# Three of four feed-forward blocks by seven half-size products, masks on VectorE, and a 72-row key tile

## The reference

```python
hm = rms_norm(h, g_mlp[l])                                              # first stack
h = h + jnp.square(jax.nn.relu(hm @ w_mlp_in[l])) @ w_mlp_out[l]
...
f = jnp.square(jax.nn.relu(h @ w_ff1[l])) @ w_ff2[l]                    # second stack
x = x + rms_norm_2(f, g_post_ffn[l])
...
mask = qi[:, None] >= k_idx[None, :]                                    # first stack's attention
s = jnp.where(mask, s, -jnp.inf)
...
logits = jnp.einsum('bqhd,bsd->bqhs', iqb, ik32) * (IDX_DIM ** -0.5)    # second stack's index
score = jnp.einsum('bqh,bqhs->bqs', iwb, jax.nn.relu(logits))
```

## Time and profile before

| | us |
|---|---|
| median of 3 runs | 2446.92 (2445.26 to 2449.81) |
| the profiled execution, whole | 2444.17 |
| its span, first to last instruction | 2442.4 |
| PE busy | 2388.9 (98% of the span), 11562 matmuls |
| DVE busy | 1342.5 (55%) |
| ACT busy | 900.2 (37%) |
| POOL busy | 350.1 (14%) |
| granted TensorE clock, mean | 0.996 |

### The profile page before, as it was taken

The page is one execution under the profiler, slowest core; times in us unless marked ns, Lnnn a source line. Parts: engine busy times, 40 slices in busy tenths (PEclk is TensorE's granted clock), DMA queues, the critical chain, the costliest instruction groups (busy, mean ns, idle before and its releaser), DMA issues.

```text
span 2442.4 us, 29077 instructions
## 1 busy us (share of the span) xinstructions
PE 2388.9 (98%) x11562; PEld 1937.8 (79%) x11562; DVE 1342.5 (55%) x1992; ACT 900.2 (37%) x1307; POOL 350.1 (14%) x270
## 2 busy tenths in 40 slices
PE   8998999999999899999999999999999999999997
PEld 6877888888887688888876878888886787888886
DVE  7765433445777643334578866334357975533433
ACT  4555332234455532223433364233233245321331
POOL 2002000002200200000146621000012742000002
PEclk9999999999999999999999999999999999999999
DMA  4211222222322123222222221222231211222221
GB/s 158 104 61 69 90 100 93 97 104 87 102 89 76 68 92 104 86 103 87 104 79 73 79 74 57 100 103 89 100 120 57 70 70 70 84 89 103 89 100 52
DMA packets 33181, 215.58 MB, mean 88 GB/s; under 512 B 4144, under 2 KB 4400, under 8 KB 8112
## 3 DMA queue, kind: packets, MB, share of 16 engines
...
## 4 chain that ended last, share of the span: by engine, by line
PE 89%; DVE 6%; ACT 2%; POOL 1%; issue 1%; DMA 0%; POOLq 0%; SPq 0%; DVEq 0%; ACTq 0%
PE ps L427 81%; DVE wl L367 1%; DVE gl L649 1%; PE ps L2257 1%; PE ps L2212 1%; PE ps L2290 1%; PE ps L2268 1%; PE ps L1390 1%; PE ps L607 1%; PE ps L1414 1%; PE ps L1377 1%; PE ps L310 1%; ACT wh L361 1%; POOL wl L408 0%; DMA wr<-in_weights 0%
## 5 line engine op out<-in xcount | busy, mean ns | idle before, releaser
L427 PE MATMUL ps<-gh,wh 128*128 128x512 f32 x1488 | 590.0, 396 | 14.0 <-DVE gl L649 11.2
L427 PE MATMUL ps<-gl,wh 128*128 128x512 f32 x1488 | 581.4, 391 | 0.0
L427 PE MATMUL ps<-gh,wl 128*128 128x512 f32 x1488 | 581.3, 391 | 0.0
L427 PE MATMUL ps<-hh,wh 128*128 128x512 f32 x1456 | 574.6, 395 | 3.4 <-ACT arena L965 1.1
L361 ACT ACTIVATE wh<-wr 128x2048 fp32r<-128x2048 f32 x184 | 351.0, 1908 | 595.1 <-PE ps L427 594.4
L427 PE MATMUL ps<-hh,wl 128*128 128x512 f32 x1456 | 567.0, 389 | 0.0
L427 PE MATMUL ps<-hl,wh 128*128 128x512 f32 x1456 | 566.8, 389 | 0.0
L367 DVE TENSOR_TENSOR wl<-wr,wh 128x2048 fp32r<-128x2048 f32 x168 | 387.0, 2304 | 278.6 <-ACT wh L361 276.4
L427 PEld LDWEIGHTS ps<-gh,wh 128*128 128x128 f32 x1488 | 279.9, 188 | 82.6 <-DVE gl L649 12.7
L427 PEld LDWEIGHTS ps<-hh,wh 128*128 128x128 f32 x1456 | 272.6, 187 | 69.4 <-issue 8.7
L427 PEld LDWEIGHTS ps<-gh,wl 128*128 128x128 f32 x1488 | 279.8, 188 | 60.0
...
## 6 DMA issues: line engine op xcount, KB each, us to landing
...
```

Of the source, the lines that this page charges most:

```text
L427: done = pe.matmul(out, stationary, moving, start=(first and n == 0), stop=(last and n == 2), skip_group_check=True)
```

## The change

Three of the four second products of every feed-forward part (FAST) are done by Strassen's scheme in its form with 15 additions. A chunk of such a product (1024 rows x 256 outputs) is taken as a 2 x 2 matrix of quarters: the upper and lower output half, and the even and odd slices of the hidden units. The hidden units are halved in positions as well, 256 each. Instead of eight products of half size seven are made ("forms"), of 4 slice pairs x 3 passes = 12 matmuls of 256 columns each, 84 in all. For them:

- GpSimd makes four sums of quarters of the raw weight chunk (sum_weights: four 128 x 512 instructions), and at the end of a chunk adds what is shared to three quarters of the output (carry: three 128 x 256 instructions).
- ScalarE and VectorE split seven forms of 128 x 512 per chunk (form_high, form_low) where they split one chunk of 128 x 2048; the eight places of a quarter chunk in wh and wl go round.
- In the first product the hidden units get four sums per pair of slices, each split too. VectorE's order there becomes even_low, rectify, other_sums, odd_low, sums_low.
- The seven results lie in half banks of PSUM and are combined by six VectorE instructions of 256 columns (first_partial, second_partial, add_quarter four times) and one of ScalarE (copy_first).

The fourth block and all first products keep their 24 matmuls of 512 columns per tile. Loops over the blocks become written-out code.

The diagonal mask of the first stack becomes two tensor_tensor_reduce of 128 x 128 on VectorE ahead of the maxima; the bf16 identity and its cast go. In the second stack the index key is computed once, in one tile of 72 rows with the index weights. VectorE copies the key out (raw_keys) and TensorE writes it twice by two products with the identity (copy_keys, at the third slice of the next tile); the transposition moves to the sixth slice and the index products start at the second slice of the tile after it.

```diff
+SUM_OF_FORM = (None, 1, 2, 3, 0, None, None)
+RAW_OF_FORM = (0, None, None, None, None, 1, 2)
...
+def sum_weights(pool, mem, sem, c):
+    g, raw, sums = sem.stage.nth_fast(c), raw_parts(mem, sem, c), weight_sums(mem, sem, c)
+    pool.wait_ge((sem["loaded0"], sem["loaded1"])[c % 2], 16 * (c // 2 + 1))
+    if g >= 2:
+        pool.wait_ge(sem["low"], split_count(c - 2))
+    pool.tensor_tensor(sums[:, 0, :], raw[:, 3, :], raw[:, 2, :], ALU.add).then_inc(sem["weight_sums"], 1)
+    pool.wait_ge(sem["weight_sums"], 4 * g + 1)
+    pool.tensor_tensor(sums[:, 1, :], sums[:, 0, :], raw[:, 0, :], ALU.subtract).then_inc(sem["weight_sums"], 1)
+    pool.wait_ge(sem["weight_sums"], 4 * g + 2)
+    pool.tensor_tensor(sums[:, 2, :], raw[:, 1, :], sums[:, 1, :], ALU.subtract).then_inc(sem["weight_sums"], 1)
+    pool.tensor_tensor(sums[:, 3, :], raw[:, 0, :], raw[:, 3, :], ALU.subtract).then_inc(sem["weight_sums"], 1)
...
+def form_high(act, mem, sem, c, forms):
+    g = sem.stage.nth_fast(c)
+    for f in forms:
+        if f == 0:
+            act.wait_ge((sem["loaded0"], sem["loaded1"])[c % 2], 16 * (c // 2 + 1))
+        slot_free(act, sem, sem.start(c) + f)
+        if SUM_OF_FORM[f] is not None:
+            act.wait_ge(sem["weight_sums"], 4 * g + SUM_OF_FORM[f] + 1)
+        act.activation(sem.form(c, f)[0], weight_form(mem, sem, c, f), ACT.Copy)            .then_inc(sem["high" if f == FORMS - 1 else "form_high"], 1)
...
+def hidden_forms_high(act, mem, sem, tile, k, j):
+    value, source, wide = mem.tmp[:, 2 + k % 2, :], mem.tmp[:, k % 2, :], S if k % 2 else HALF
+    act.wait_ge(sem["drained"], tile + 1)
+    act.activation(value, source, ACT.Square).then_inc(sem["hidden_high"], 1)
+    act.activation(mem.hh[:, k, 0:wide], source[:, 0:wide], ACT.Square).then_inc(sem["hidden_high"], 1)
...
+def even_low(dve, mem, sem, p):
+    k, even = 2 * (p % PAIRS), mem.tmp[:, 2, :]
+    dve.wait_ge(sem["hidden_high"], 4 * p + 2)
+    dve.tensor_tensor(mem.hl[:, k, 0:HALF], even[:, 0:HALF], mem.hh[:, k, 0:HALF].bitcast(F32), ALU.subtract).then_inc(sem["hidden_low"], 1)
+    dve.tensor_tensor(even[:, 0:HALF], even[:, HALF:S], even[:, 0:HALF], ALU.subtract).then_inc(sem["hidden_sums"], 1)
+def other_sums(dve, mem, sem, p):
+    even, odd, sums = mem.tmp[:, 2, :], mem.tmp[:, 3, :], mem.sums
+    dve.wait_ge(sem["hidden_high"], 4 * p + 3)
+    dve.wait_ge(sem["hidden_sums"], 4 * p + 1)
+    dve.tensor_tensor(sums[:, 0:HALF], odd[:, HALF:S], even[:, 0:HALF], ALU.subtract).then_inc(sem["hidden_sums"], 1)
+    dve.tensor_tensor(sums[:, HALF:S], odd[:, HALF:S], even[:, HALF:S], ALU.subtract)
+    dve.wait_ge(sem["hidden_sums"], 4 * p + 2)
+    dve.tensor_tensor(sums[:, S:S + HALF], odd[:, 0:HALF], sums[:, 0:HALF], ALU.subtract).then_inc(sem["hidden_sums"], 1)
...
+    order = (("x", "b11", True), ("z", "t2", True), ("t", "b22", True), ("v", "t3", True), ("y", "t1", True),
+             ("x", "b21", False), ("v", "t4", False))
+    def ready(f):
+        if f == FORMS - 1:
+            pe.wait_ge(sem["low"], split_count(c))
+        else:
+            pe.wait_ge(sem["form_low"], (FORMS - 1) * g + f + 1)
+        if f == 0 and g >= 2:
+            pe.wait_ge(sem["combined"], 6 * (g - 2) + 5)
+        if f in (1, 2, 3, 4) and g >= 1:
+            pe.wait_ge(sem["combined"], 6 * (g - 1) + (1, 2, 6, 4)[f - 1])
+        if f == 5:
+            pe.wait_ge(sem["copied_first"], g + 1)
+        if f == 6:
+            pe.wait_ge(sem["combined"], 6 * g + 3)
+    def part(f, q):
+        place, name, fresh = order[f]
+        if q == 0:
+            ready(f)
+        if first and name == "b11":
+            pe.wait_ge(sem["hidden_low"], KT * j + 2 * q + 1)
+        elif first and name in ("b21", "b22"):
+            pe.wait_ge(sem["hidden_low"], KT * j + 2 * q + 2)
+        elif first:
+            pe.wait_ge(sem["hidden_sums"], 4 * (PAIRS * j + q + 1))
...
+    late = (1, 2, 3, 4) if first else ()
+    for f in range(5):
+        for q in range(PAIRS - (f in late)):
+            part(f, q)
+    for f in late:
+        part(f, PAIRS - 1)
+    for f in (5, 6):
+        for q in range(PAIRS):
+            part(f, q)
...
+def carry(pool, mem, sem, g, target):
+    u = mem.partial[:, g % 2]
+    pool.wait_ge(sem["combined"], 6 * (g + 1))
+    for row, part, n in ((0, slice(HALF, S), 1), (1, slice(HALF, S), 1), (1, slice(0, HALF), 0)):
+        last = pool.tensor_tensor(target[row][:, part], target[row][:, part], u[:, n, :], ALU.add)
+    last.then_inc(sem["carried"], 1)
...
+def fast_block_dve(dve, mem, sem, c0, j, tile_of, split_ahead, bank, target):
+    for i in range(BC):
+        p = PAIRS * j + i
+        rectify(dve, mem, sem, tile_of[c0 + i], 2 * i, bank=bank(tile_of[c0 + i]))
+        even_low(dve, mem, sem, p)
+        rectify(dve, mem, sem, tile_of[c0 + i] + 1, 2 * i + 1, bank=bank(tile_of[c0 + i] + 1))
+        if i < 2 and split_ahead:
+            split_low(dve, mem, sem, c0 + i + 2)
+        if i == 2:
+            form_low(dve, mem, sem, c0 + BC, range(4))
+        other_sums(dve, mem, sem, p)
+        if i == 3:
+            form_low(dve, mem, sem, c0 + BC, (4,))
+        odd_low(dve, mem, sem, p)
+        sums_low(dve, mem, sem, p)
+    for oc in range(BC):
+        g, c = BC * j + oc, c0 + BC + oc
+        rows = target(2 * oc), target(2 * oc + 1)
+        ahead = oc + 1 < BC
+        if oc == 0:
+            form_low(dve, mem, sem, c, (5, 6))
+        first_partial(dve, mem, sem, g)
+        if oc:
+            form_low(dve, mem, sem, c, (6,))
+        add_quarter(dve, mem, sem, g, "t", 3, rows[0][:, HALF:S])
+        add_quarter(dve, mem, sem, g, "v", 4, rows[1][:, HALF:S])
+        if not ahead:
+            split_low(dve, mem, sem, c + 1)
+        second_partial(dve, mem, sem, g)
+        if ahead:
+            form_low(dve, mem, sem, c + 1, (0, 1))
+        add_quarter(dve, mem, sem, g, "x", 6, rows[0][:, 0:HALF])
+        if ahead:
+            form_low(dve, mem, sem, c + 1, (2,))
+        add_quarter(dve, mem, sem, g, "v", 7, rows[1][:, 0:HALF])
+        if ahead:
+            form_low(dve, mem, sem, c + 1, (3, 4, 5))
+        else:
+            split_low(dve, mem, sem, c + 2)
+def fast_block_pool(pool, mem, sem, c0, j, target):
+    def rows(oc):
+        return target(2 * oc), target(2 * oc + 1)
+    sum_weights(pool, mem, sem, c0 + BC)
+    for oc in range(BC):
+        if oc + 1 < BC:
+            sum_weights(pool, mem, sem, c0 + BC + oc + 1)
+        carry(pool, mem, sem, BC * j + oc, rows(oc))
...
-            dve.tensor_copy(mem.idb[:, :], cst[:, C_ID:C_ID + P]).then_inc(shared["cast"], 1)
...
-            own.mark(dve.tensor_reduce(small[:, SM_MAX + 2 * b:SM_MAX + 2 * b + 2], ps[:, 2 + 2 * b:4 + 2 * b, 0:n], AX.X, ALU.max))
+            for c in range(2):
+                edge = ps[:, 2 + 2 * b + c, n - P:n]
+                own.mark(dve.tensor_tensor_reduce(edge, edge, mem.trib, 1.0, NEG, ALU.add, ALU.max,
+                                                  small[:, SM_MAX + 2 * b + c:SM_MAX + 2 * b + c + 1]))
             own.settle()
+            if n > P:
+                own.mark(dve.tensor_reduce(small[:, SM_MAX + 2 * b:SM_MAX + 2 * b + 2], ps[:, 2 + 2 * b:4 + 2 * b, 0:n], AX.X, ALU.max))
+                own.settle()
...
                 half = slice(DH * c, DH * (c + 1))
-                pe.matmul(ps[:, 2 + 2 * b + c, 0:n], qk[half, h, P * i:n], qk[half, 4 + h, 0:n], start=True, stop=False,
-                          skip_group_check=True)
-            for c in range(2):
-                last = pe.matmul(ps[:, 2 + 2 * b + c, n - P:n], mem.idb[:, :], mem.trib, start=False, stop=True,
+                last = pe.matmul(ps[:, 2 + 2 * b + c, 0:n], qk[half, h, P * i:n], qk[half, 4 + h, 0:n], start=True, stop=True,
                                  skip_group_check=True)
...
-        rotate_first(4, 4, ik, sem["index_rotated"], sem["index_swapped"])
-        dve.wait_ge(sem["product"], 6)
+        dve.wait_ge(sem["product"], 5)
+        dve.tensor_copy(raw_keys, ps[0:DH, b_bank(4), :]).then_inc(sem["drained"], 1)
         dve.wait_ge(sem["index_rotated"], 4)
-        dve.tensor_tensor(tmp[0:HEADS2, 3, :], ps[0:HEADS2, b_bank(5), :], mem.rb[0:HEADS2, :], ALU.mult)\
-            .then_inc(sem["drained"], 1)
+        rows = slice(DH, DH + HEADS2)
+        dve.tensor_tensor(tmp[rows, 3, :], ps[rows, b_bank(4), :], mem.rb[rows, :], ALU.mult).then_inc(sem["index_weights"], 1)
+        rotate_first(5, 4, ik, sem["index_rotated"], sem["index_swapped"])
 
...
-        product_tile(pe, mem, sem, B_IKW, P, 5, mem.gh, mem.gl, width=HEADS2, bank=b_bank(5))
+        product_tile(pe, mem, sem, B_IKW, 0, 4, mem.gh, mem.gl, width=DH + HEADS2, bank=b_bank(4))
+
+        def copy_keys():
+            pe.wait_ge(sem["drained"], 5)
+            for e in range(2):
+                last = pe.matmul(ps[DH * e:DH * (e + 1), b_bank(5), :], ident[0:DH, 0:DH], raw_keys, start=True, stop=True,
+                                 skip_group_check=True)
```

(31 more changed lines are left out.)

295 lines of the change are left out of this document (214 added, 81 removed).

## The result

The changed kernel takes 2494.47 us (median of 4; 2491.39 to 2496.87) against 2448.36 for the kernel before on the same chip: ratio 1.0194, 95% interval 1.0182 to 1.0206. It is slower, as forecast, but by 46 us, where the forecast of 2471 is 23 above the same median, and it lies just above the range.

The account below looks back on a forecast made before the run. PE was taken as the bound (89% of the chain of waits). Terms -38.4 + 31 + 12 + 24 - 4.3 + 1.4 - 0.1 = +25.6 gave 2469.8, or 2472.5 from the median: forecast 2471 us, range 2427 to 2494.

Parts of the forecast that it names:

- the first number: Fast second products: matmuls 0.120 us apart at 256 columns, 0.2267 at 512, so 10.08 us a chunk, not 10.88; -38.4 us.
- three signs: Wrong if PE's named idle times sum under 40 us, VectorE keeps 0.4 beside sums, or 256-column spacing leaves 0.115 to 0.125.
- second product, 48 chunks: Three blocks of four chunks in four layers: 0.80 us saved per chunk if PE never waits, -38.4 us.
- eight later blocks: Fast blocks after each layer's first: PE waits 1.5 us at pair 3 and 1.5 elsewhere, 3.0 a block, +24 us.
- first block, first stack, two: First-stack layers' first blocks: pair 3's low half 4.5 us late, the rest 1.5; 6.0 each, +12 us.
- first block, second stack, two: Second-stack layers' first blocks: PE waits 8.0 us for tile 6's bank, 5.6 at pair 3; 15.5 a layer, +31 us.
- masks: First-stack diagonal masks moved to VectorE: one 0.7 us wait counted in each layer, +1.4 us; bounds -0.5 to +8.
- the key tile: Index key in second-stack layers: -4.0 us in the folded layer, -0.3 in the other, together -4.3; bounds -9.6 and +3.
- taking turns: VectorE instructions on SBUF operands and GpSimd's sums exclude each other; each such VectorE instruction waits up to 1.24 us.
- cover is enough: Rival: GpSimd's sums do not hold up VectorE where it matters; -19.0 us, 2425 to 2428; chance 0.27.
- Heavier blocking: Rival: each fast block loses 5 to 6 us, as carries and sums also displace form_low; 2495 to 2505; chance 0.12.
- with turns or without: Second stack's first block: pair 3's even low half 5.6 us late in either case, as the bank's wait delays PE too.

Follow-up runs that it names:

- a_arena_last: Changed kernel with the arena laid behind all other tiles, as in the kernel before: 2471.33 us, ratio 1.0098 to the kernel before.
- a_no_sums: Changed kernel with 64 bytes of padding behind the arena and GpSimd's weight sums left out (computation incomplete): 2454.78 us, against 2489.12 with the padding alone.
- a_reordered: Changed kernel with the arena behind all other tiles and helpers' and TensorE's work reordered in the fast blocks: 2422.12 us, ratio 0.9901.

## Why the prediction was wrong

**The step that failed** is the first number: "The rows show 120 and 227 for this kernel's matmuls, so my sum keeps to them." They are of that kernel's matmuls at that kernel's places. I read the diff for its instructions and did not price its allocations, so the cost of a changed distance stood in the sum as nothing. a_arena_last, which has the change without the move, takes 2471.33 against a forecast of 2471; the move takes the rest, 2494.47 - 2471.33 = 23.1: 512 columns at 0.2331, not 0.2270 (+41), and 256 columns at 0.1163, not 0.1199 (-17). None of the three signs that I had named for being wrong could show this: PE's waits grew by 45 us, VectorE took 1.49 us beside the sums, and 0.1163 lies between 0.115 and 0.125. I had set no sign on 512 columns.

**The other terms**, read in a_arena_last. PE's time from the first matmul of a fast product to the first behind it, less 40.32:

| term | forecast | measured |
|---|---|---|
| second product, 48 chunks | -38.4 | -38.4 (0.1199 us each) |
| eight later blocks | +24 | +18 (42.4 to 43.2 us a block) |
| first block, first stack, two | +12 | +14.5 (47.78, 47.37) |
| first block, second stack, two | +31 | +30 (45.67, 44.07; bank 8.1; clock 2.3) |
| masks | +1.4 | +1.6 (waits alone: those of the transposition are 10.1 us, 8.5 in the earlier trace rows) |

That the total is so near the forecast is partly luck: the terms miss by -6, +2.5, -1 and +0.2, the key tile below by +3.2, and the clock, which I left out, fills part of waits that I had made too long. The three in the middle rest on taking turns, which a_no_sums bears out. The rival "cover is enough" falls with them: its deciding wait, at pair 3 of the later blocks, is 1.4 to 2.1 us in a_arena_last, where I had 1.5.

```profile
1526.93 0.76 PE L472 MATMUL ps<-gh,wh 128*128 128x512 f32 x1 [8.09 <-DVE tmp L703]
1544.98 0.39 PE L472 MATMUL ps<-hh,wh 128*128 128x256 f32 x1 [3.61 <-DVE hl L809]
1632.04 0.39 PE L472 MATMUL ps<-hh,wh 128*128 128x256 f32 x1 [1.38 <-DVE hl L809]
```

"Heavier blocking" named nearly the time, 2495 to 2505, but not the cause: blocks of the changed kernel lose less than I had said, not more.

**The clock** I left out wholly. PE's windows in a_arena_last around the bank wait (PE busy, count, granted clock, DMA):

```profile
1516.00:1520.00 4.00, 2.84 (x13) 1.00 0.04 14
1520.00:1524.00 4.00, 0.00 (x0) 0.68 0.00 0
1524.00:1528.00 4.00, 1.07 (x3) 0.50 0.00 0
1528.00:1532.00 4.00, 4.00 (x12) 0.54 0.00 0
1532.00:1536.00 4.00, 4.00 (x19) 1.00 0.00 0
```

PE stood still from 1518.8; the granted clock fell to 0.50, the 1.2 GHz level, and was back about 4.7 us after PE went on. Eleven matmuls in between start 0.43 us apart, not 0.227: 2.2 us more. In all stretches that the trace gives at that level the large matmuls take 18 us more than at full clock, against 3 in the one before. In the block terms this hid behind waits that I had made too long.

**The key tile** in the unfolded layer is where it shows. PE waits 2.09 and 0.75 us there (4.1 forecast). But from the third matmul behind the first wait on it runs at the lower level (1886.96 and 1887.39 are 0.43 apart), and the copy takes 1.90 us from its start to the next:

```profile
1886.29 0.47 PE L472 MATMUL ps<-hh,wh 128*128 128x512 f32 x1 [2.09 <-DVE arena L2252]
...
1886.96 0.63 PE L472 MATMUL ps<-hh,wl 128*128 128x512 f32 x1
1887.39 0.63 PE L472 MATMUL ps<-hh,wh 128*128 128x512 f32 x1
...
1889.62 1.97 PE L2555 MATMUL ps<-arena,cst 64*64 64x512 f32 x4 [0.75 <-DVE arena L2262]
1891.52 0.79 PE L472 MATMUL ps<-hh,wh 128*128 128x512 f32 x1
```

From the layer's opening to its first scores (TensorE L677 at 1851.11 to L2622 at 2001.56; before, L632 at 1836.86 to L2257 at 1984.37) this layer takes 150.45 us against 147.51: +2.9, not -0.3. In a_reordered the same place looks so:

```profile
1850.07 0.47 PE L472 MATMUL ps<-hh,wh 128*128 128x512 f32 x1 [2.09 <-DVE arena L2292]
...
1853.40 1.08 PE L2595 MATMUL ps<-arena,cst 64*64 64x512 f32 x4 [1.70 <-DVE arena L2302]
1854.41 0.50 PE L472 MATMUL ps<-hh,wh 128*128 128x512 f32 x1
```

The waits are 2.09 and 1.70, the granted clock is 1.00 from 1848 to 1860, and the stretch (L677 at 1814.94 to L2662 at 1962.65) takes 147.71 us, +0.2. So most of the +2.9 is the clock, and the first wait alone does not decide whether it falls; what does, these runs leave open. In the folded layer the copy takes 1.01 us from its start to the next, as estimated (1.06). The layer's net is not measured apart.

**Two stalls in a row do not add.** In a_no_sums the second stack waits 4.0 us at pair 3 although the bank's wait is 5.5 shorter. I had seen this (5.6 "with turns or without"), and its size was too big by about 2.

What stays open: with +2.9 here and the other layer's -4.0 at its forecast, the terms sum to -38.4 + 18 + 14.5 + 30 + 1.6 + 2.9 - 4.0 = +24.6, and the medians differ by 23.1; single runs of the kernel before spread from 2443 to 2450. Why equal places within 256 bytes are best for 512 columns and worst for 256, and whether they are so at every place, was not tried. Nor was it measured by itself how many of the 34 us of a_no_sums are the turns.
